# A transformer kernel in three-pass fp32r: the order of VectorE's sums and a fourth accumulator in the block-product phases

## What is computed

```python
# first block: the MLP, 4096 hidden
hn = rms_norm(h, norm_mlp_g[l])
up = jax.nn.relu(jnp.einsum('bsd,df->bsf', hn, w_mlp_up[l]))
h = h + jnp.einsum('bsf,fd->bsd', up * up, w_mlp_down[l])
...
# second block: the feed-forward parts, 2816 hidden, two in each of two layers
x = x + 0.5 * swiglu(rms_norm_2(x, ffn1_norm[l]), ffn1_w_gate[l], ffn1_w_up[l], ffn1_w_down[l])
...
x = x + memory_cross_attention(rms_norm_2(x, xa_norm[l]), rms_norm_2(mem, mem_norm[l]),
                               xa_wq[l], xa_wkv[l], xa_wo[l])
```

## Time and profile before

| | |
|---|---|
| median of three runs | 3369.77 us (3366.86 to 3370.22) |
| profiled execution, its own time | 3368.93 us |
| its span | 3367.1 us |
| TensorE busy | 3308.0 us, 98% |
| VectorE busy | 2288.6 us, 68% |
| ScalarE busy | 1509.2 us, 45% |
| GpSimd busy | 251.2 us, 7% |
| DMA | 314.15 MB, 93 GB/s |

### The profile page before, as it was taken

How to read it: one execution, slowest core, us unless ns; L and a number is a source line. 1 busy time by engine, 2 the same in 40 slices (tenths; PEclk the granted TensorE clock), 3 DMA queues, 4 the chain that set the end, 5 groups by cost and what they waited for, 6 DMA issues and landing times.

```text
span 3367.1 us, 46615 instructions
## 1 busy us (share of the span) xinstructions
PE 3308.0 (98%) x17322; PEld 2792.2 (83%) x17322; DVE 2288.6 (68%) x3628; ACT 1509.2 (45%) x2406; POOL 251.2 (7%) x302
## 2 busy tenths in 40 slices
PE   8999999999999999999999999999999999999999
PEld 6878887888888888878888888888887788888887
DVE  5777876478877767678654677467656875457564
ACT  4455435344444444445744344344334565444343
POOL 1000000000000000038200000000000660000000
PEclk9999999999999999999999999999999999999999
DMA  4333332233233333222222333333332232223332
GB/s 145 92 86 94 99 110 82 92 112 100 90 99 92 96 101 97 83 88 88 88 88 63 93 96 100 91 103 94 99 98 84 86 101 76 76 76 96 104 98 78
DMA packets 424783, 314.15 MB, mean 93 GB/s; under 512 B 15433, under 2 KB 421377, under 8 KB 424593
## 3 DMA queue, kind: packets, MB, share of 16 engines
q1 hardware_dynamic: 421264, 301.77, 29.9%
q0 software_dynamic: 2896, 8.49, 0.8%
q10 hardware_dynamic: 432, 1.38, 0.1%
HBM read 309.46 MB, written 2.13 MB: 93 GB/s over the span
## 4 chain that ended last, share of the span: by engine, by line
PE 81%; DVE 9%; issue 4%; POOL 3%; ACT 2%; DMA 0%; DVEq 0%; SPq 0%; POOLq 0%; ACTq 0%
PE G L789 61%; PE G L838 6%; POOL arena L3268 3%; DVE w_lo L2330 2%; PE G L1034 2%; PE G L1011 2%; PE B L838 1%; PE B L778 1%; DVE h L2395 1%; DVE arena L2343 1%; PE G L730 1%; PE B L709 1%; PE B L1034 1%; PE B L681 1%; DVE w_lo L2312 1%
## 5 line engine op out<-in xcount | busy, mean ns | idle before, releaser
L1458 ACT ACTIVATE w_hi<-raw 128x1024 fp32r<-128x1024 f32 x421 | 445.7, 1059 | 878.5 <-PE G L789 795.3
L2312 DVE TENSOR_TENSOR w_lo<-raw,w_hi 128x1024 fp32r<-128x1024 f32 x422 | 521.9, 1237 | 443.7 <-ACT w_hi L1458 441.8
L789 PE MATMUL G<-y_hi,w_hi 128*128 128x512 f32 x1824 | 720.6, 395 | 0.3 <-DVE w_lo L2312 0.2
L789 PE MATMUL G<-y_hi,w_lo 128*128 128x512 f32 x1824 | 710.4, 389 | 0.0
L789 PE MATMUL G<-y_lo,w_hi 128*128 128x512 f32 x1824 | 710.0, 389 | 0.0
L789 PE MATMUL G<-xn_hi,w_hi 128*128 128x512 f32 x1504 | 591.9, 394 | 1.4 <-DVE w_lo L2312 1.4
L789 PE MATMUL G<-xn_hi,w_lo 128*128 128x512 f32 x1504 | 585.6, 389 | 0.0
L789 PE MATMUL G<-xn_lo,w_hi 128*128 128x512 f32 x1504 | 585.4, 389 | 0.0
L789 PEld LDWEIGHTS G<-y_hi,w_hi 128*128 128x128 f32 x1824 | 342.4, 188 | 80.4 <-issue 9.0
L789 PEld LDWEIGHTS G<-y_lo,w_hi 128*128 128x128 f32 x1824 | 342.6, 188 | 73.9 <-issue 4.3
L789 PEld LDWEIGHTS G<-y_hi,w_lo 128*128 128x128 f32 x1824 | 342.4, 188 | 71.8
(11 more groups left out here) (546 smaller groups left out, 5500.4 us busy)
## 6 DMA issues: line engine op xcount, KB each, us to landing
raw<-in_w_in SPq DMA_DIRECT2D x128, 512.0 KB, 4.4
raw<-in_ffn_w_gate SPq DMA_DIRECT2D x88, 512.0 KB, 4.0
raw<-in_ffn_w_up SPq DMA_DIRECT2D x88, 512.0 KB, 5.2
raw<-in_ffn_w_down SPq DMA_DIRECT2D x64, 512.0 KB, 4.1
raw<-in_w_mlp_up SPq DMA_DIRECT2D x32, 512.0 KB, 4.6
raw<-in_w_mlp_down SPq DMA_DIRECT2D x32, 512.0 KB, 4.3
raw<-in_xa_wkv SPq DMA_DIRECT2D x32, 512.0 KB, 4.4
raw<-in_w_out SPq DMA_DIRECT2D x24, 512.0 KB, 4.3
```

Source lines behind the costliest of these rows:

```text
L789: m = pe.matmul(bank[:, 0:n], a[:, k, kt, :], b[:, kt * S:kt * S + n], start=(kt == tiles[0] and t == 0), stop=(kt == tiles[-1] and t == 2))
L1458: act.activation(weights_part(w_hi, n + 1, k), raw_part(n + 1, k), ACT.Copy).then_inc(s_whi, 1)
L2312: dve.tensor_tensor(weights_part(w_lo, n + 1, k), raw_part(n + 1, k), weights_part(w_hi, n + 1, k).bitcast(F32), ALU.subtract).then_inc(s_ ...
```

## The change

Block products: there is a fourth accumulator w. ScalarE copies z into w after MIX3, MIX4 adds to w, and VectorE's evacuation of z comes after that copy. x and extra now come from the four B banks in turn, y, z and w are G banks. The sums S1 and S2 have a second buffer for odd pairs. The four sums of pair 0 are made at the end of the last pair but one of the up phase; sums S1 and S3 of pair 1 in the last pair of the up phase, behind low S1 (which in `swiglu` moves behind the first reading of G). Pair 0 of VectorE's `blocks` gets the order of the other pairs. The normalization of the memory is spread over one pair more.

```diff
-        block_sums = {S1: arena[:, 19 * T:20 * T], S2: arena[:, 14 * T:15 * T], S4: arena[:, 15 * T:16 * T]}
+        block_sums = {S1: (19, 16), S2: (14, 17), S4: (15, 15)}
...
             late = (P0[name] - 1) % 2
-            x = G[2 * (1 - late) + 1] if i % 2 == 0 else B[BANK.get(("blocks", name, i), 0)]
-            return x, G[2 * late], G[2 * late + 1], G[2 * (1 - late)]
+            x, extra = (B[BANK.get((key, name, i), 0)] for key in ("blocks", "extra"))
+            return x, G[2 * (1 - late)], G[2 * late], G[2 * late + 1], extra
...
                     n, every = P0[name] + i, range(nk // 2)
-                    if i == 0:
-                        pe.wait_ge(s_free, n - 1)
-                    if i % 2:
-                        take(("blocks", name, i), (gone_v, (name, i, "x")))
-                    elif i:
-                        pe.wait_ge(gone_v.sem, gone_v.at(name, i - 2, "x"))
-                    x, y, z, extra = accumulators(name, i)
+                    take(("blocks", name, i), (gone_v, (name, i, "x")))
+                    take(("extra", name, i), (gone_v, (name, i, "q22")))
+                    x, y, z, w, extra = accumulators(name, i)
...
                     pe.wait_ge(op_v.sem, op_v.at(name, i, S1))
-                    if i:
-                        pe.wait_ge(gone_v.sem, gone_v.at(name, i - 1, "q22"))
                     product(i, MIX1, extra, every, True)
...
                     pe.wait_ge(s_wlo, 2 * n + 2)
-                    pe.wait_ge(gone_v.sem, gone_v.at(name, i, "z"))
-                    product(i, MIX4, z, every, False)
-                pe.wait_ge(gone_v.sem, gone_v.at(name, 3, "q22"))
+                    pe.wait_ge(seed_a.sem, seed_a.at(name, i, "w"))
+                    product(i, MIX4, w, every, False)
+                pe.wait_ge(gone_v.sem, gone_v.at(name, 3, "y"))
...
             def seed(name, i, which):
 
-                x, y, z, _ = accumulators(name, i)
-                act.wait_ge(block_p.sem, block_p.at(name, i, FIRST if which == "y" else MIX2))
-                if which == "y" and i:
-                    act.wait_ge(gone_v.sem, gone_v.at(name, i - 1, "y"))
+                x, y, z, w, _ = accumulators(name, i)
+                act.wait_ge(block_p.sem, block_p.at(name, i, {"y": FIRST, "z": MIX2, "w": MIX3}[which]))
+                if which == "w" or i == 0:
+                    act.wait_ge(s_free, P0[name] + i - (which == "y"))
                 else:
-                    act.wait_ge(s_free, P0[name] + i)
-                act.activation((y if which == "y" else z)[:, 0:HALF], x[:, 0:HALF], ACT.Copy)\
+                    act.wait_ge(gone_v.sem, gone_v.at(name, i - 1, which))
+                dst, value = {"y": (y, x), "z": (z, x), "w": (w, z)}[which]
+                act.activation(dst[:, 0:HALF], value[:, 0:HALF], ACT.Copy)\
                    .then_inc(seed_a.sem, seed_a.mark(name, i, which))
...
                     for x in range(3):
+                        if x == 1:
+                            seed(name, i, "w")
                         if i < 3:
                             operand_hi(name, i + 1, (A11, S1, S2)[x])
...
-                if i == 4:
+                if i == 3:
                     root(3, MEM)
...
                     operand_lo(name, i, A22)
                     if i:
                         next_sum(name, i, S3)
-                        evacuate_y(i, y)
-                        next_lo(name, i, 0)
-                        next_sum(name, i, S2)
-                    dve.wait_ge(block_p.sem, block_p.at(name, i, MIX3))
+                    else:
+                        mix_lo(name, KTS[name] // 2 - 1, D14, last_mix(name))
+                    evacuate_y(i, y)
+                    next_lo(name, i, 0)
+                    next_sum(name, i, S2)
+                    dve.wait_ge(seed_a.sem, seed_a.at(name, i, "w"))
                     evacuate(i, z, 1, 1, -1.0, "q22").then_inc(gone_v.sem, gone_v.mark(name, i, "z"))
-                    if i == 0:
-                        mix_lo(name, KTS[name] // 2 - 1, D14, last_mix(name))
-                        next_lo(name, i, 0)
-                        next_sum(name, i, S1)
-                        evacuate_y(i, y)
-                        next_sum(name, i, S3)
-                        next_lo(name, i, 1)
-                        next_sum(name, i, S2)
-                    else:
-                        next_lo(name, i, 1)
+                    next_lo(name, i, 1)
...
             def first_operands(name, at_):
 
-                if at_ == 0:
+                if at_ == -1:
                     for m in (S1, S3, S2, S4):
                         operand_sum(name, 0, m)
+                if at_ == 0:
                     operand_lo(name, 0, A11)
                 if at_ == 1:
                     operand_lo(name, 0, S1)
+                    operand_sum(name, 1, S1)
+                    operand_sum(name, 1, S3)
...
                         for kind_ in (D12, D12O, D32, D14):
                             mix_lo(down, i, kind_, mlp_mix(i))
+                        if i == NPAIR[name] - 2:
+                            first_operands(down, -1)
...
                         mix_lo(down, i // 2, D12, values)
-                        first_operands(down, 1)
                         dve.wait_ge(s_free, n)
                         product(n, 0)
                         dve.tensor_tensor(tmp(q), G[2 * q][:, :], rstd[:, :], ALU.mult).then_inc(s_ao, 1)
+                        first_operands(down, 1)
                         product(n, 1)
...
+                    if down and i == NPAIR[name] - 2:
+                        first_operands(down, -1)
...
-                if i == 5:
+                if i == 4:
                     norm_rstd(3, MEM, mem_rstd)
-                    link(dve.tensor_tensor(memn.rearrange("p (j m) -> p j m", j=KT), mem_t.rearrange("p (j m) -> p j m", j=KT),
-                                           mem_rstd[:, None, :].to_broadcast([P, KT, MEM]), ALU.mult))
+                if i in (5, 6):
+                    half = slice(4 * (i - 5) * MEM, 4 * (i - 4) * MEM)
+                    link(dve.tensor_tensor(memn[:, half].rearrange("p (j m) -> p j m", j=KT // 2),
+                                           mem_t[:, half].rearrange("p (j m) -> p j m", j=KT // 2),
+                                           mem_rstd[:, None, :].to_broadcast([P, KT // 2, MEM]), ALU.mult))
```

More of the change, by code:

```diff
@@ L520, in operand @@
             if m in block_sums:
-                return block_sums[m][:, 0:nk // 2 * P].rearrange("p (k c) -> p k c", c=P)
+                at_ = block_sums[m][n % 2] * T
+                return arena[:, at_:at_ + nk // 2 * P].rearrange("p (k c) -> p k c", c=P)
             rows, cols = {A11: (0, 0), S3: (0, 1), A12: (1, 0), A22: (1, 1)}[m]
@@ L2416, in last_of @@
                     dve.wait_ge(s_mm, 2 * (P0[name] + i) + 2)
-                    evacuate(i, accumulators(name, i)[2], 1, 0, -1.0, None).then_inc(s_free, 1)
+                    evacuate(i, accumulators(name, i)[3], 1, 0, -1.0, None).then_inc(s_free, 1)
                 for i in range(4):
-                    x, y, z, extra = accumulators(name, i)
+                    x, y, z, _, extra = accumulators(name, i)
                     if i:
```

## The result

| | before | after |
|---|---|---|
| median of four runs each | 3368.32 us (3365.73 to 3370.22) | 3341.66 us (3341.03 to 3344.72) |
| profiled execution, its own time | 3368.93 us | 3341.49 us |
| its span | 3367.1 us | 3339.4 us |
| granted TensorE clock, mean | 0.997 | 0.999 |

The ratio is 0.9923 [0.9906, 0.994]: 0.8% faster. The forecast was 3347.0, its range began at 3342.5.

A forecast was written before the change was run, and what follows sets the result against it. TensorE, busy 98% of the span, was taken as the bound, so only its waits could go. Stalls -25.7, MLP sums +3.6 and memory -0.7 gave -22.8 us: 3368.93 to 3346.1, raised 0.84 to 3347.0; range 3342.5 to 3353.

The forecast's parts named there:

- Fourth accumulator: MIX4 of pairs 1 and 2, every block phase: waits go, 1.32 + 0.31 us; copy 0.38 after MIX3, margin 0.66.
- ScalarE is idle there: Copy of z into w: argument against it coming too late for MIX4, a slower outcome given chance 0.03.
- Seed in time: MIX2 of pair 1, every block phase: earlier S2 lets ScalarE's seed y come in time, saving 0.71 us.
- MLP phases: Start of the three MLP phases: two sums on late VectorE delay MIX2 of pair 0, +1.21 us a phase.
- Feed-forward gap: Between G's two readings before eight feed-forward phases: two sums take 1.21 of VectorE's 2.04 us idleness, costing nothing.
- the list of signs: Expected trace signs, including VectorE's idleness before G's second reading falling from 2.04 to about 0.8 in a feed-forward phase.
- Memory: Second up phase: halving the 128x2048 multiplication over two pairs removes TensorE's stall behind it, -0.7 us once.
- VectorE behind the copy: z's evacuation, each pair: waits for the copy, starting 0.79 instead of 0.32 after MIX3; the 0.47 us is hidden.
- Rival 3: Sums cost less and small restarts go too (second matmul of MIX1, pair 1): 3342.5 us, chance 0.10.
- The numbers: Whole kernel: forecast's own spread +-1.5 us, range 3342.5 to 3353; faster means below 3363.0, chance 0.94.

The follow-up runs named there:

- the last version: Changed kernel with MLP sums S1 and S3 of pair 1 made inside pair 0 and the fourth phase's normed tile between G's two readings; 3339.09 us, ratio 0.9916.

## Why the prediction was off by 5.3 us

**Right.**
- Fourth accumulator: MIX4 waits nowhere, the copy starts 0.32 after the last start of MIX3 (forecast 0.38) and has 0.72 to spare (0.66) in pairs 1 to 3. In pair 0 it starts 0.54 to 0.62 after it and has 0.43 to 0.54 to spare: "ScalarE is idle there" does not hold in that pair, and the margin was wide enough.
- Seed in time: MIX2 of pair 1 on the pitch. Forecast for both together 2.34 a feed-forward phase, measured 2.35 to 2.37 in six of them, 2.46 in the fourth and 2.64 in the eighth. These contain the restarts named below; the three stalls alone gave 2.30.
- MLP phases: +1.19 to +1.21 each in pair 0, forecast +1.21. MIX2 of pair 0 is 1.62 late, forecast 1.6. Undoing it gave 1.08 back. Net of the gains a phase fell by 1.23 (44.20 to 42.97, forecast 43.1).
- Feed-forward gap: the two sums cost nothing. The idleness left is 0.85 to 1.06 in seven of the eight, forecast about 0.8, and 0.26 in the fifth phase, behind the memory's second half. The paragraph on the memory had counted that phase rightly (VectorE through by 1286.9, its next operand at 1287.1); the list of signs, with its 0.8 for "a feed-forward phase", had not.
- Memory: -0.74, forecast -0.7.
- VectorE behind the copy: in pairs 0 to 2 it reaches z 0.26 to 0.73 after the copy's end, so the 0.47 that I had counted as hidden does not arise. In pair 3 it waits 0.40 for the copy, and that is hidden, as counted. On two engines at one bank no run says anything, since every kernel here kept that wait.

**A term mis-sized.** The sum said 22.8 and the block phases with the memory's stall give 23.7. The 0.9 are restarts of 0.07 to 0.11 us at the second matmul of MIX1 of pair 1, in all eleven phases, 0.95 together, with another 0.03 to 0.04 at the first in five of them, and 0.21 in pair 0 of the eighth phase, less 0.4 by which the eleven times three stalls were smaller than 2.34. They had no row of their own among the waits. Rival 3 had named just this term and priced it at 0.9; it belonged in the sum, since the late VectorE behind it was the one that the change relieves: with the new order alone the restart is gone, with the old order and the accumulator it stays (0.10 in all eleven).

**The step that failed: "The numbers".** "The forecast's own spread is +-1.5 (the runs of before span 3.4 us)." The sum was hung on a profiled time of 3368.93 and then raised to the median of three runs, 3369.77. The kernel before ran another 50 times in these experiments: median 3366.85, from 3363.6 to 3372.37. The anchor was 2.9 us high, and the spread of one kernel's runs is 8.8 us, not 3.4; stretches at half clock, whose length changes from run to run, had no term in the sum and no part in the range. With the anchor and the restarts put right, 3347.0 - 2.9 - 0.9 = 3343.2.

What makes that spread can be read. The runs differ by their mean granted clock, and the profiles show the clock fall to half behind idle stretches of TensorE, for 3 to 11 us at a place, and in some executions not at all. One fall does not fit: in the trace with the normed tile it comes at 1437.7, 21 us behind the nearest idleness of more than 0.9 us. Means of the 50 runs of before (one more of them, 3363.6, had 1.000) and of the changed kernel's 14:

```
mean clock    before             after
0.999         3365.51 (9 runs)   3341.42 (8 runs)
0.998         3366.32 (22)       3343.3  (5)
0.997         3367.89 (10)       3343.86 (1)
0.996         3370.73 (8)        none
```

At equal clock the kernels are 24.1, 23.0 and 24.0 us apart, which is the 23.7 of the phases and the memory's stall. The medians over all runs (3366.85 and 3341.78) are 25.1 apart. The other 1.4 go with the changed kernel's runs lying at the higher clocks more often (8 of 14 at 0.999, against 9 of 50): if the runs of before were spread over the clocks like those of the changed kernel, their mean would be 3365.97, which is 23.7 above the other's mean, 3342.26. Why they lie there is not settled. It may be the chips: 32 of the 50 runs of before are from one chip, with 5 at 0.999, and the changed kernel's ten runs in the experiments are from two others, on the first of which it is 4 of 9 against 3 of 5. It may be the kernel, which comes to the idle stretches at another moment: the versions differ (all four runs of the accumulator alone at 0.998, four of five of the last version at 0.997). Or it may be luck.

The two ends of the range were thus built from mechanisms alone. Rival 3's 3342.5 was worked out from the same anchor, and 3341.66 lies below it though half of what rival 3 says (that the MLP sums cost nothing) is false. What is left of the miss when the anchor and the restarts are put right, 3343.2 against 3341.66, is about these 1.4 us, whose cause stays open.

## What to carry to other kernels

Before a sum of a few tenths of a per cent is hung on a median, ask what one kernel's runs differ by, and look for it in the trace: here three runs put the anchor 2.9 us off, more than every mis-sized term of the sum together. Two halves of a change may each look worthless or partial alone (by the phases the order costs 2.5, the accumulator brings 16.5, both bring 23.7), because the wait that one frees is only moved until the other takes its condition away. When an effect is smaller than the scatter, judge by the phase lengths of the profile, and by medians only at equal clock: the kernel with GpSimd's sums had the lower median and the longer phases.

## What was not expected of the hardware

- GpSimd's sum of 128x512 in fp32 took 1.74 to 1.80 us, VectorE's 0.68, and VectorE's operation with two SBUF operands, begun beside it, ended 0.55 after GpSimd's both times (1.78 and 1.07 us instead of 0.68), while the one that reads PSUM ran at 0.68.
- Behind the same 2.61 or 2.62 us of idleness, at two places in each of twelve traces, the half clock lasted 6.8 us four times, 3.4 us fifteen times, and five times there was none. It differed between executions of one kernel.
- A wait costs more than its length: the start after the matmul that ends it comes 0.07 to 0.11 late, and such a restart also appears behind waits too short to be listed (0.95 us in eleven phases).
